# A hybrid layer with a product-key expert mixer: the first product of one sample tile from gathered rows, other dots moved, some low parts on GpSimd

## The reference, cut to what matters

```python
s_top, i_top = lax.top_k(s, PEER_TOPK)          # per token, 8 heads, two halves of a key
...
best, pos = lax.top_k(cand_s, PEER_TOPK)        # 16 experts of 16384 per head: 128 per token
gate = jax.nn.softmax(best, axis=-1)
def block(args):
    xt, it, gt = args
    a = jax.nn.gelu(jnp.einsum('td,tkd->tk', xt, u_tab[it]))
    return jnp.einsum('tk,tkd->td', gt * a, v_tab[it])
```

## Time and profile before

| what | value |
|---|---|
| median of 3 runs (lowest, highest) | 2248.36 us (2241.95, 2249.47) |
| the profiled execution's own time | 2244.61 us |
| its span, first to last instruction | 2242.8 us |
| PE busy | 2154.6 us, 96% of the span |
| DVE, ACT, POOL busy | 62%, 37%, 23% |
| DMA, mean over the span | 212 GB/s |

### The profile page before, as it was taken

How to read it: one execution, slowest core, us unless ns; L and a number is a source line. 1 busy time by engine, 2 the same in 40 slices (tenths; PEclk the granted TensorE clock), 3 DMA queues, 4 the chain that set the end, 5 groups by cost and what they waited for, 6 DMA issues and landing times.

```text
span 2242.8 us, 28983 instructions
## 1 busy us (share of the span) xinstructions
PE 2154.6 (96%) x9868; PEld 1664.0 (74%) x9868; DVE 1388.6 (62%) x2919; ACT 834.1 (37%) x1506; POOL 508.7 (23%) x329
## 2 busy tenths in 40 slices
PE   6999999698998999999999999999999999999998
PEld 2554455445997787788888888887888888888886
DVE  4221425423889999677777777226666666666665
ACT  2111003323212222677877877223222223223222
POOL 0000001002324555333333332003222222222120
PEclk8999999798999999999999999999999999999999
DMA  9121114305102444488888887747888888888883
GB/s 338 53 75 45 73 43 178 150 1 197 56 21 85 169 136 142 160 307 317 322 319 315 317 319 293 285 139 281 315 298 284 290 293 285 293 283 296 279 298 132
DMA packets 179297, 475.50 MB, mean 212 GB/s; under 512 B 16263, under 2 KB 50215, under 8 KB 176648
## 3 DMA queue, kind: packets, MB, share of 16 engines
q1 hardware_dynamic: 142344, 340.20, 42.7%
q0 software_dynamic: 36864, 134.23, 17.9%
HBM read 401.76 MB, written 72.61 MB: 212 GB/s over the span
## 4 chain that ended last, share of the span: by engine, by line
PE 90%; DVE 4%; DMA 2%; ACT 1%; issue 1%; POOL 1%; SPq 0%; POOLq 0%; DVEq 0%; ACTq 0%
PE ps L965 30%; PE ps L906 29%; PE ps L624 5%; PE ps L946 5%; PE ps L717 3%; PE ps L843 3%; PE ps L878 3%; PE ps L879 3%; PE ps L683 2%; DMA wring<-in_w_ada 1%; PE ps L623 1%; PE ps L636 1%; DMA ain<-gelu_scratch 1%; PE ps L742 1%; PE ps L743 1%
## 5 line engine op out<-in xcount | busy, mean ns | idle before, releaser
L906 PE MATMUL ps<-h2hi,uhi 128*128 128x512 f32 x1024 | 446.3, 436 | 18.5 <-DVE scores L1375 7.7
L965 PE MATMUL ps<-vhi,whi 128*128 128x512 f32 x1024 | 400.8, 391 | 8.1 <-DVE wlo L1465 8.1
L906 PE MATMUL ps<-h2hi,ulo 128*128 128x512 f32 x1024 | 402.8, 393 | 0.0
L906 PE MATMUL ps<-h2lo,uhi 128*128 128x512 f32 x1024 | 401.1, 392 | 0.0
L965 PE MATMUL ps<-vlo,whi 128*128 128x512 f32 x1024 | 400.2, 391 | 0.0
L965 PE MATMUL ps<-vhi,wlo 128*128 128x512 f32 x1024 | 399.9, 391 | 0.0
L1751 ACT ACTIVATE vhi<-vraw 128x1024 fp32r<-128x1024 f32 x128 | 135.5, 1061 | 471.4 <-PE ps L965 464.0
L1835 POOL DMA_INDIRECT vgat<-in_v_tab,idx x128 | 151.4, 1183 | 659.7 <-DVE y L1475 507.7
L1463 DVE TENSOR_TENSOR vlo<-vraw,vhi 128x1024 fp32r<-128x1024 f32 x128 | 156.9, 1226 | 215.8 <-ACT vhi L1751 215.8
L1827 POOL DMA_INDIRECT ugat<-in_u_rows,idx x128 | 176.9, 1382 | 287.4 <-DVE dots L1427 265.4
L1417 DVE TENSOR_TENSOR ulo<-uraw,uhi 128x1024 fp32r<-128x1024 f32 x87 | 106.7, 1226 | 200.8 <-ACT uhi L1672 200.8
(11 more groups left out here) (268 smaller groups left out, 2998.0 us busy)
## 6 DMA issues: line engine op xcount, KB each, us to landing
uraw<-in_u_t SPq DMA_DIRECT2D x128, 512.0 KB
vraw<-in_v_tab SPq DMA_DIRECT2D x128, 512.0 KB, 5.2
gelu_scratch<-aout SPq DMA_DIRECT2D x128, 256.0 KB
gate_scratch<-gst SPq DMA_DIRECT2D x16, 2048.0 KB
ain<-gelu_scratch SPq DMA_DIRECT2D x128, 256.0 KB, 4.2
gin<-gate_scratch SPq DMA_DIRECT2D x32, 1024.0 KB, 9.4
wring<-in_w_ada SPq DMA_DIRECT2D x12, 2048.0 KB, 9.3
wring<-in_w_in SPq DMA_DIRECT2D x6, 2048.0 KB, 8.3
```

The source lines that it names most:

```text
L906: last = pe.matmul(ps[:, b % 4, :], w[:, b % 2, k, :], h[:, k, LP:T], start=(k == 0 and j == 0), stop=(k == KD - 1 and j == 2))
L965: last = pe.matmul(ps[:, y_bank(t) + h, :], w[:, b, (t - 1) * P:t * P], v[:, b, h * 512:(h + 1) * 512], start=(start and j == 0), stop=(st ...
```

## The change

- **The first product of the last sample tile** (tile 4, `TU`) is no longer computed by PE: all 128 first products have 384 columns (`TA`) in place of 512. Its 128 rows of `u` per token are gathered and its dots taken by DVE, 128 over the first 45 blocks of B (three a block, two in every sixth or so). The gelu of the dots times the gate is turned by PE once and goes into the one-hots of that tile, so its gate matrix holds gate times gelu and needs no `weight` in stretch 2 (line 1459 now has 384 columns, too).
- **The prompt's 128 dots** follow: two a block in the last 19 blocks of B, three a block in C (74 in all), and the remaining 54 in the first 36 blocks of stretch 2, three in two blocks. The additions of `v` rows start at block 39 of stretch 2, 128 over 89 blocks.
- `BLK_A` is 52, so A has 52 blocks and C 12. POOL starts gathers after 24 blocks. DVE does tile 4's choice of keys and experts first, then tile 0's.
- **Every second low part** of stretch B goes from DVE to POOL (`pool_low`).
- The gelus are stored with 384 columns and loaded for four blocks at once; loops of stretch 2 are written out.

The core of the diff:

```diff
-BLK_A = 40
+TU = NT - 1
+TA = TD - P
+BLK_A = 52
-DOTS_IT = DOTS_B * NB_B
-POOL_FROM = 8
+POOL_FROM = 24
+NDOT = 2 * HK
+U_LAST = 44
+DOTS_C = 3
+def dots_before(n):
+    m = n - BLK_A
+    if m <= U_LAST:
+        return -(-HK * m // (U_LAST + 1))
+    if n <= BLK_C:
+        return HK + DOTS_B * (m - U_LAST - 1)
+    d = dots_before(BLK_C)
+    if n <= NBLK:
+        return d + DOTS_C * (n - BLK_C)
+    return min(NDOT, d + DOTS_C * (NBLK - BLK_C) + 3 * (n - NBLK) // 2)
+
+def pool_low(n):
+    return BLK_A < n <= BLK_C and n % 2 == 0
...
-                        last = pe.matmul(ps[:, b % 4, :], w[:, b % 2, k, :], h[:, k, LP:T],
+                        last = pe.matmul(ps[:, b % 4, 0:TA], w[:, b % 2, k, :], h[:, k, LP:LP + TA],
...
-                    if k == 4:
+                    if k == 4 and not pool_low(n + 1):
+                        dve.wait_ge(ulo_ready, n + 1)
                         split_u(n + 1, n + 1)
-                if m % NB_B == 2 and m >= NB_B:
-                    slot_weights(m // NB_B - 1)
-                for e in range(DOTS_B):
-                    dot(DOTS_B * m + e)
-            for n in range(BLK_C + 1, NBLK):
-                split_u(n, n)
+                if m == TURN_U:
+                    slot_weights(0)
+                for g in dots_at(n):
+                    dot(g)
+            dve.wait_ge(ulo_ready, BLK_C + 1)
+            for n in range(BLK_C, NBLK):
+                if n + 1 < NBLK:
+                    split_u(n + 1, n + 1)
+                for g in dots_at(n):
+                    dot(g)
...
+            act.wait_ge(h2lo_ready, NT)
+            wait_unit(act, "hp1")
+            for h in range(2):
+                move(f"hp{h}", h2turn[:, h * 512:(h + 1) * 512])
...
-                act.activation(aout[:, b % 4], ps[:, b % 4, :], ACT.Gelu_apprx_tanh).then_inc(gelu_done, 1)
+                act.activation(aout[:, b % 4], ps[:, b % 4, 0:TA], ACT.Gelu_apprx_tanh).then_inc(gelu_done, 1)
...
-            for n in range(NTD * NB_B):
-                if n:
-                    for e in range(DOTS_B):
-                        gather_u(DOTS_B * (n - 1) + e + GSLOT)
+            pool.wait_ge(idx_ready, 2)
+            for n in range(BLK_A, BLK_C):
+                if pool_low(n + 1):
+                    pool.wait_ge(ulo_ready, n + 1)
+                    split_u(n + 1, n + 1, False)
+                for g in dots_at(n):
+                    gather_u(g + GSLOT)
+            for g in range(dots_before(BLK_C) + GSLOT, NDOT):
+                gather_u(g)
```

More of the change, by code:

```diff
@@ L265, in bass_hybrid_layer @@
             order += {"mix": [f"mx0{t}", f"mx1{t}"], "turn": [f"tr2_{t}0", f"tr2_{t}1"], "ada": [f"ada{t}"]}[kind]
-        order += ["adc10", "adc11", "hr0", "hr1"]
+        order += ["adc10", "adc11"] + [f"h{x}{h}" for x in "up" for h in range(2)]
         for h in range(HP):
@@ L416, in bass_hybrid_layer @@
         v_landed = [sem(f"v_landed{b}") for b in range(4)]
[L417 removed]
+        a_landed = [sem(f"a_landed{b}") for b in range(2)]
         g_landed = [sem(f"g_landed{b}") for b in range(2)]
@@ L854, in _ @@
                 ada_cols(i)
-            for h in range(2):
-                transposes(f"hr{h}", [h2T[:, 4 * h + j, 0:P] for j in range(4)])
+            for x, t in (("u", TU), ("p", 0)):
+                for h in range(2):
+                    transposes(f"h{x}{h}", [h2T[:, 4 * h + j, rows(t)] for j in range(4)])
             pe.wait_ge(ld_keys, 16)
@@ L1389, in _ @@
                     best_keys(t, h)
-            for t in range(1, NT):
+            dve.wait_ge(h2row_ready, 1)
+            for x, t in enumerate((TU, 0)):
+                best_experts(t)
+                seq(dve.scalar_tensor_tensor(work[:, 9], selw[:, t, 0], float(NKEYS), selw[:, t, 1], ALU.mult, ALU.add))
+                dve.tensor_copy(idxs[:, x], work[:, 9]).then_inc(idx_ready, 1)
+            for t in range(1, TU):
                 best_experts(t)
@@ L1476, in add_value @@
+            def add_value(g):
+                s = g % GSLOT
+                dve.wait_ge(v_gathered[s], 16 * (g // GSLOT + 1))
+                if g == 0:
+                    dve.wait_ge(w0_ready, 2)
+                    dve.tensor_scalar(y0[:], vgat[:, s], dots[:, 1, 0:1], None, ALU.mult).then_inc(v_added, 1)
+                else:
+                    dve.wait_ge(v_added, g)
+                    dve.scalar_tensor_tensor(y0[:], vgat[:, s], dots[:, 1, g:g + 1], y0[:], ALU.mult, ALU.add
                                              ).then_inc(v_added, 1)
-            def step_2(it, first, last):
-                for b in range(TOPK):
-                    n = it * TOPK + b
-                    if not (last and b == TOPK - 1):
-                        weight(it, b + 1)
-                    low_parts(n, b % R2)
-                    add_value(it, b, first)
@@ L1486, in _ @@
-            slot_weights(NTD - 1)
-            weight(0, 0)
-            step_2(0, True, False)
-            with dve.Fori(1, IT_2 - 1) as it:
-                step_2(it, False, False)
-            step_2(IT_2 - 1, False, True)
+            weight(0)
+            for n in range(NBLK):
+                if n + 1 < NBLK:
+                    weight(n + 1)
+                low_parts(n)
+                for g in dots_at(NBLK + n):
+                    dot(g)
+                if n == GELU_P + 1:
+                    slot_weights(1)
+                for g in values_at(n):
+                    add_value(g)
@@ L1730, in _, with step_b @@
                 pair(n, n % 4, False, False)
-            def step_b(it, first, second):
+            def step_b(it, first):
                 for b in range(NB_B):
@@ L1735, in step_b @@
                     split_u(n + 1, b + 1, False)
-                    if b == 0 and not first:
-                        slot_gelu(it - 1, second)
+                    if n == BLK_A + GELU_U:
+                        slot_gelu(0)
                     if n + 1 < BLK_C:
```

185 lines of the change are left out of this document (100 added, 85 removed).

## The result

| | before | after |
|---|---|---|
| median of 7 runs (lowest, highest) | 2243.87 us (2241.95, 2249.47) | 2267.19 us (2257.99, 2272.51) |
| profiled execution, its span | 2244.61, 2242.8 us | 2265.43, 2263.6 us |
| PE, DVE, ACT, POOL busy | 96, 62, 37, 23% | 91, 69, 36, 35% |
| PE's granted clock | 0.979 | 0.951 |

The ratio is 1.0092, with a 95% interval of 1.0074 to 1.011. The change makes the kernel 0.9% slower; the forecast was 1.7% faster, and the range ended at 2252 us.

The account below looks back on a forecast made before the run. The prediction took PE as the kernel's bound. Its terms, 31 for A, -17 for B, -56 for C and 3 more, summed to -39 us, giving a median of 2209 us, 1.7% less; range 2125 to 2252 us.

Parts of the forecast that it names:

- PE's floor in B is 6.08 us: Stretch B: PE alone would need 6.08 us a block, gate matmuls included, so 389 us for 64 blocks.
- Stretch A, the loop through ACT and POOL, 266 us: Stretch A: gelu, high part and POOL's low part set the pace, 4.99 then 4.50 us a block; 266 us, 31 more.
- The handover to B: End of stretch A: from ACT's table load to the first gate block, 15 us with shorter blocks, 15.9 before.
- Nearly every block was to show PE idle ahead of its first matmul: Stretch A, expected sign: PE idle until POOL's low part releases it, with blocks of 4.5 to 5.0 us.
- POOL's low part and DVE wait for each other, 1.0 a block: Stretch B: POOL's low part and DVE's dots block each other; 1.0 us a block taken, between 0 and 1.2.
- 0, if it falls on one-hots (one tensor input): Stretch B: lower bound of the POOL and DVE mutual wait, no cost if the low part runs beside one-hots.
- First 45 blocks of B: DVE, 7.43: First 45 blocks of B: DVE's one-hots, dots, half a low part and mutual wait make 7.43 us a block, 334 us.
- rival 2: From B on: DMA is the bound, ceiling 333 to 365 GB/s; at 333, 26 us slower, 2274 us; chance 0.12.
- Stretch C: DMA, 75 us: Stretch C and preloads: DMA moves 31.4 MB at 425 GB/s; 75 us, 56 less than before.
- Rival 3: B and C: a DMA ceiling of 365 GB/s, 542 us for both, 27 us faster in all, 2221 us; chance 0.1.
- Stretch 2, "within 5 us": Stretch 2: matmuls kept, DVE's 4.3 us a block hidden under PE's 5.44; within 5 us of 714.
- What would make it wrong: Signs: B at 6.1 to 6.5 us, gathers landing after 7 us or more, clock falling in A, PE idling in stretch 2.

Follow-up runs that it names:

- the two versions with all fixes: Changed kernel with six slots, gates stored in four parts, one dot a block in C; B's low parts all on DVE, 2173.51 us, or every second on POOL, 2186.32 us.
- the last version: Changed kernel with six slots, four gate parts, one dot a block in C, B's low parts on DVE, C's gate stores and preloads spread over blocks: 2159.14 us.
- six slots, all fixes but the last: Changed kernel with six slots, gates stored in four parts, one dot a block in C and all low parts of B on DVE: 2173.51 us, ratio to before 0.9675.

## Why the prediction was wrong

- **"PE's floor in B is 6.08 us"**: right, 5.99 where nothing else holds it. The slope drawn from 512 and 320 columns carried to 384.
- **Stretch A, the loop through ACT and POOL, 266 us**: the right engines, 15 us too long, and the loop was built wrongly. With two buffers the halves of block n+1 wait for the end of product n-1, not of product n, so the 4.50 us come round once in two blocks and the block between costs PE's own 4.16. ACT's gelus, one at the end of each product, show it:

```profile
717.59 0.49 ACT L1752 ACTIVATE aout<-ps 128x384 f32<-128x384 f32 x1 [2.72 <-PE ps L949]
...
722.05 0.49 ACT L1752 ACTIVATE aout<-ps 128x384 f32<-128x384 f32 x1 [3.02 <-PE ps L949]
...
726.21 0.49 ACT L1752 ACTIVATE aout<-ps 128x384 f32<-128x384 f32 x1 [2.72 <-PE ps L949]
...
730.76 0.49 ACT L1752 ACTIVATE aout<-ps 128x384 f32<-128x384 f32 x1 [3.06 <-PE ps L949]
...
734.95 0.49 ACT L1752 ACTIVATE aout<-ps 128x384 f32<-128x384 f32 x1 [2.75 <-PE ps L949]
```

  The steps are 4.46, 4.16, 4.55 and 4.19, with low parts of 2.40 on POOL. The forecast's own terms give (4.50 + 4.16)/2 = 4.33 a block, where it took 4.50, and it took 4.99 while DVE chooses. The low part was also shorter then than its 2.889; from 740 to 900 us:

```profile
L1880 POOL TENSOR_TENSOR ulo<-uraw,uhi 128x1024 fp32r<-128x1024 f32 x34 | 90.0, 2648 | 61.6 <-ACT uhi L1742 61.5
```

  The first 50 blocks ended at 920.6 and took 230 us, 21 less than forecast, though the four gathers cost one step 8 us (forecast: 5). The handover to B took 20 us, 5 more. PE's longest wait for `ulo`, 6.1 us, is the stall at the gathers. Nearly every block was to show PE idle ahead of its first matmul; the trace shows only 6 such waits between 700 and 900, 9.1 us in all, since every second block has no gap and the modelled ends of the matmuls cover one of some 0.3 us.
- **"POOL's low part and DVE wait for each other, 1.0 a block"**: right in size (1.06), wrong in place. The bound "0, if it falls on one-hots (one tensor input)" is false: 72% of it falls there, and 54% (38 of 71 us) between the two versions with all fixes. Eight one-hots took 4.80 us at 1065.33 while POOL's low part ran (1066.63 to 1069.01); they take 2.2. The Trainium skill says so, "SBUF — State Buffer", Who interferes with whom: a `tensor_scalar` from and to SBUF can enter a mode that uses both of DVE's ports, and then contends with POOL, too. By that sentence one-hots are no safe place; the trace agrees (460 ns for 359). The forecast had drawn on the same section for the pair of two-input products.
- **"First 45 blocks of B: DVE, 7.43"** is the step that failed. The last of tile 4's dots starts at 1328, so these blocks took 387 us, 8.6 each, in place of 334, and the last 19 took 131 in place of 120. DVE's own work was costed well: without gathers all of B takes 442 us (forecast: 454). The term that is missing is DVE's wait for gathered rows, 56 us in these 45 blocks. I had written it down, "Gathers would then land later than DVE asks: four slots, one dot every 2.6 us", but under rival 2, as something that only a DMA ceiling brings. It needs no ceiling. Four slots at 2.6 us give a slot's round 10.4 us. Its own dot takes 1.26 of them, so 9.1 are left from the end of a dot to the start of the dot four places on. Landing, counted from where POOL takes up the gather, takes 6.9 at the median in B and up to 16.4, with up to two gathers and every second block a low part of 2.6 ahead of it on POOL: the median fits, the high values don't. The trace of before has no landing times for rows of `u`; what it shows is that no dot waited with two dots a block, when four slots held two blocks, 14.7 us. That bounds the round trip from above only. But it has them for the gathers of `v` rows in stretch 2, as large as those of `u`:

```profile
DMA to landing us min/median/max: 4.1/5.1/9.8
```

  The longest is over 9.1 even with nothing ahead of it on POOL. The change cuts the time below a bound that had been measured, so the wait was an unknown cost, and its row for `v` spoke against zero; it was left out of the sum and the forecast's own range.
- **"Stretch C: DMA, 75 us"**: 93.7, with DMA busy for 98% at 374 GB/s. Two terms were mis-sized, for about half of the miss each. C moved 35.0 MB, not 31.4: the two last gate stores of 2 MB go out in it and stand nowhere in the sum. And the forecast's 425 came from single slices of 7.5 us; no version carried it over a whole stretch. With one dot a block C takes 75.3, and 63.3 in the last version.
- **Rival 2**, slower through a ceiling of 333 to 348 GB/s, would have had the right sign, and its mechanism isn't what the runs show: the last version moves 368 GB/s over all of B. Rival 3, a ceiling at 365, falls with it. The same holds for the 358 of the Trainium skill, "SBUF — State Buffer", Summary: rules for kernel authors; the trace does not agree with it for this kernel on one core. The DMA share, 0.84 before at 307 GB/s and 0.96 at 368, is near its end, though.
- **Stretch 2, "within 5 us"**: right, 703.2 for 707.4. Its dots wait 11 us for gathers, hidden.
- **What would make it wrong**: the text named "dots wait on gathers that land after 7 us or more", which is what happened. The granted clock fell as well, in B and C; in A it went from 0.99 to 0.97 only.

Open: how much of B's loss the lower clock carries by itself. B's matmuls are 31 us longer in busy time than without gathers (426.2 for 394.9), but most of that may lie beside DVE's waits. The clock in B stays at 1.00 without gathers and at 0.99 in the last version, so it falls where the waits are. More than six slots, and gathers issued ahead of the low part on POOL, weren't tried.

## What to carry to other kernels

A stream with slots is bound by its round trip as well as by its rate: slots times the consumer's period has to hold the slot's release, the issue queue ahead of it and the landing time *under load*, with its high values, and a mean bandwidth with room to spare says nothing of that. When a change moves work to an engine that was waited for by nobody, cost the waits that its old slack paid for: here DVE's 105.6 us of idle time in B, and a period that gave each slot 14.7 us. And where several fixes sit behind one wait, judge them together: low parts on DVE instead of POOL were worth nothing that one run shows while gathers were late, and 13 us of the whole once they weren't.

## What the runs showed of the hardware

- One-hots with one tensor input and a POOL low part hold each other up: a mean of 460 ns with it, 359 without.
- A gather of 512 KB lands after 4.8 us at best and 16.4 at worst in the changed kernel, and its median grows with the number of slots: 6.6, 7.3 and 8.1 us with three, four and six (of `v` rows before the change, 5.1).
- A PE that was busy for 0.38, 0.00 and 0.43 us in three stretches of 2 us from 1080 had a clock of 1.00, 0.66 and 0.50 in them and 0.50 in the next, in which it was at work. Waiting for late transfers in C gave 0.82 on average with PE busy for 65% of the time.
- A load of 512 KB issued right behind four stores of 1 MB on the same queue landed after 18.8 us, where the median of the kernel (six slots, all fixes but the last) is 6.5, and ACT waited 12.85 us for it. With the stores spread the longest such wait in C was 4.7 us.
